# Float32r list matmuls, and the first two row gathers issued in the routing block

## The chip, the cores and the metric

One NeuronCore of a Trainium2 chip runs the whole program. The metric is the device time of one execution in microseconds (us); lower is better. The kernel before takes 1667.98 us, the median of 3 runs (1664.65 to 1668.8).

## The reference, cut to what matters

A two-layer decoder trunk for 512 tokens of width 1024. Each layer has a mixer (layer 0: retention and pooling; layer 1: sparse attention over selected keys), a layer norm, a mixture of 32 experts with exact top-2 dispatch, a layer norm, and a gated injection. The change lies in the dispatch of the mixture of experts, which each layer does once:

```python
g_logits = (xt @ w_group) + b_group            # 4 groups, top 1
e_logits = (xt @ w_expert) + b_expert          # 8 experts in the group, top 2
gate     = g_w[:, None] * softmax(top_v)
expert   = grp[:, None] * EXPERTS_PER_GROUP + top_i
order    = argsort(flat_e)                     # (token, expert) pairs by expert
...
h = xt[tok] @ w_gu[e];  a, b = split(h, 2)     # per block of rows of one expert
ys = (silu(a) * b) @ w_down[e]
y  = zeros.at[row_tok].add(ys * row_gate)      # back to the tokens
```

All of it is float32. The lists (which token rows an expert reads, and where its results go) are whole numbers.

## The kernel before, in words

The program is a row of blocks. In a block each engine has its own stream of instructions, and semaphores order them. A block closes with a barrier of all engines: GpSimd (POOL) collects the arrivals of the other four engines and then releases them; after it, POOL alone clears the semaphores of earlier blocks (L79, `Stages.end`), and the next block starts. So an engine that arrives late, POOL too, holds all others.

For each layer `layer_end` calls two blocks, `route(l)` and `experts(l, ...)`:

- **`route`** makes the lists. VectorE (DVE) picks group and experts from the router's logits, and forms a membership matrix; TensorE (PE) turns it into ranks with bf16 matmuls (L737 to L741). DVE then writes, for 8 columns `u` of pairs, a one-hot matrix RS of the rank (L829, 128x1024) and the table VALUES of token numbers (L818). Eight matmuls (L746) of 128x128 stationary RS and 128x64 moving VALUES, both float32, add up in the PSUM bank MP the rows that each slot of each expert takes (32 columns) and puts (32 columns). DVE copies them as integers to `rows` (L844), whose halves are the views `taken` and `put`. POOL has only two memsets in this block (L761, L762), ready long before. SyncE (SP) issues the load of the third expert's down weights (L442).
- **`experts`** goes through the 32 experts in 16 pairs, q = 0 and 1. For each expert POOL copies its column of `taken` to a small tile (L1337) and issues an indirect DMA that gathers its rows of x from the HBM tensor `x_rows` (L871): 128 half rows of 2 KB, 64 slots, where empty slots read nothing. PE transposes them (L883), ScalarE (ACT) copies the result (L917), PE multiplies with gate and up weights (L898, 32 records per expert), ACT and DVE form the gated product (L921, L924), PE transposes and multiplies with the down weights (L905, L912), ACT scales (L1477), and POOL scatters the result (L877).

At the start of `experts`, POOL issues the gathers of experts 0 and 1, then an indirect DMA that blanks a part (L1352), waits for DVE's list of further rows, and enters its loop. PE starts with eight float32 matmuls (L1409, RS by GATES) that give each slot's gate, and only then does it wait for the first gather and transpose it. DVE waits for these gates before `list_further` (L935 to L953) and further list work (L1055, L1058).

The weights come over SP's one DMA queue: 4 MB of gate and up weights (two halves) and 2 MB of down weights for each expert. There are three areas for them. The first three experts' weights are issued ahead, in the blocks before; the load for expert 3 waits until PE has read the first half of expert 0's weights (`gu_after(0, 3, 0, 1)`), and from there on each load waits for PE to be through with the weights that it replaces.

Of the kernel before, what the change touches and what calls it, by code (L numbers as in the profile page):

```python
# [13 lines left out]
F32 = mybir.dt.float32  # L14
F32R = mybir.dt.float32r
# [3 lines left out]
ALU = mybir.AluOpType  # L19
# [3 lines left out]
P = 128  # L23
SEQ = 512
D = 1024
T = SEQ // P
# [11 lines left out]
NE = NG * EPG  # L38
# [12 lines left out]
def build(nc, A, out):  # L51
    ctx = ExitStack()
    ctx.enter_context(nc.allow_non_contiguous_dma(reason="small vectors to one feature per partition"))
    with ctx:
        def sb(name, shape, dt=F32):
            return ctx.enter_context(nc.sbuf_tensor(name, shape, dt))

        def lasting(name):

            return ctx.enter_context(nc.semaphore(name))  # L60
# [21 lines left out]
        sem = Stages.new  # L82
# [4 lines left out]
        def three(ap, b):  # L87
            return ap.rearrange("p (a b) -> p a b", b=b)
# [3 lines left out]
        w2 = sb("w2", [P, 4096])  # L92
# [9 lines left out]
        half_col = sb("half_col", [P, 2])  # L102
# [510 lines left out]
        R = route_views()  # L613
# [91 lines left out]
        CP = PS[0:1, 3, 0:NE]  # L705
        MP = PS[:, 5, 0:2 * NE]
        GP = PS[:, 7, 0:NE]
        RS = three(w2[:, 3072:3072 + 2 * T * P], P)
        VALUES = three(w2[:, 1024:1024 + 2 * T * 2 * NE], 2 * NE)
        GATES = three(w2[:, 2048:2048 + 2 * T * NE], NE)  # L710

        def over_tiles(ap, n):

            return ap.rearrange("p (o e) -> p o e", o=1).broadcast_to([P, n, ap.shape[1]])

        def over_columns(ap, n):

            return ap.rearrange("p (t o) -> p t o", o=1).broadcast_to([P, ap.shape[1], n])

        def route(l):  # L720
            n = f"route{l}"
            s_gmax, s_gexp, s_diff, s_ex = sem(f"{n}_gmax"), sem(f"{n}_gexp"), sem(f"{n}_diff"), sem(f"{n}_ex")
            s_member, s_rank = sem(f"{n}_member"), sem(f"{n}_rank")
            s_values, s_slots = sem(f"{n}_values"), sem(f"{n}_slots")
            s_zero = sem(f"{n}_zero")
            with nc.Block() as block:
                @block.sync
                def _(sp):
                    load_third_dn(sp, l)

                @block.tensor
                def _(pe):

                    pe.wait_ge(s_member, 1)
                    for t in range(T):
                        for u in range(t):
                            pe.matmul(RK[:, t, :], ones[:, :], R["M"][:, u, :], start=(u == 0), stop=False)  # L737
                        m = pe.matmul(RK[:, t, :], tri[:, :], R["M"][:, t, :], start=(t == 0), stop=True)
                    m.then_inc(s_rank, 1)
                    for t in range(T):  # L740
                        m = pe.matmul(CP, ones[:, 0:1], R["M"][:, t, :], start=(t == 0), stop=(t == T - 1))  # L741
                    m.then_inc(s_rank, 1)

                    pe.wait_ge(s_values, 1)
                    for u in range(2 * T):
                        m = pe.matmul(MP, RS[:, u, :], VALUES[:, u, :], start=(u == 0), stop=(u == 2 * T - 1))  # L746
                    m.then_inc(s_slots, 1)

                @block.scalar
# [9 lines left out]
                @block.gpsimd  # L759
                def _(pool):  # L760
                    pool.memset(w2[:, 0:1024], 0.0).then_inc(s_zero, 1)  # L761
                    pool.memset(R["zeros"], 0.0).then_inc(s_zero, 1)  # L762
                    pool.wait_ge(s_zero, 2)

                @block.vector
                def _(dve):
                    own = Own(dve, f"{n}_own")
# [55 lines left out]
                    for j in range(2):  # L823
# [2 lines left out]
                    own.wait()  # L826
                    pos = R["pos"].rearrange("p j t -> p (j t)")
                    own.done(dve.tensor_reduce(pos, R["rank"], AX.X, ALU.add))
                    dve.tensor_tensor(RS, over_tiles(R["slot"], 2 * T), over_columns(pos, P), ALU.is_equal)\  # L829
                       .then_inc(s_values, 1)  # L830

                    dve.wait_ge(s_gexp, T)
# [8 lines left out]
                    own.mark(dve.tensor_copy(entry[:, :, 2], gates))  # L841

                    dve.wait_ge(s_slots, 1)
                    own.mark(dve.scalar_tensor_tensor(R["rows"], MP, 2.0,  # L844
                                                      half_col[:, 1:2].broadcast_to([P, 2 * NE]), ALU.mult, ALU.add))
                    own.wait()
            Stages.end()


# [13 lines left out]
        def wait_alone(eng, semaphore, value, tick):  # L863


            eng.wait_ge(semaphore, value)
            eng.sem_inc(tick, 1)

        def gather(pool, q, index, s):

            pool.indirect_dma_start(out=xg[q], out_offset=None, in_=x_half,  # L871
                                    in_offset=bass.IndirectOffsetOnAxis(ap=index, axis=0),
                                    bounds_check=2 * SEQ - 1, oob_is_err=False).then_inc(s, 16)
# [177 lines left out]
        def place_last(dve, own, e, placed):  # L1051

            OH, W = R["OH"], R["last"]
            for t in range(T):
                own.mark(dve.tensor_scalar(W[:, t, :], RS[:, t, :], OH[:, t, e:e + 1], None, ALU.mult))  # L1055
            own.wait()
            for t in range(T):
                own.mark(dve.scalar_tensor_tensor(W[:, t, :], RS[:, T + t, :], OH[:, T + t, e:e + 1], W[:, t, :],  # L1058
                                                  ALU.mult, ALU.add))
# [189 lines left out]
                            xs = X[:, t - 2, c * NB:(c + 1) * NB]  # L1249
                            dve.tensor_tensor(xs, xs, sig[u % 4], ALU.add).then_inc(self.s_done, 1)  # L1250

        def experts(l, inj):

            n = f"moe{l}"
# [13 lines left out]
            def both(name, new=sem):  # L1270
                return [new(f"{n}_{name}{q}") for q in range(2)]

            s_take, s_gath, s_turn, s_xe = both("take"), both("gath", lasting), both("turn"), both("xe")
            s_gu_half = both("gu_half")
            s_gu, s_silu, s_gated, s_gturn = both("gu"), both("silu"), both("gated"), both("gturn")
            sp_tick, pool_tick = sem(f"{n}_sp_tick"), sem(f"{n}_pool_tick")
# [6 lines left out]
            with nc.Block() as block:  # L1283
# [47 lines left out]

                @block.gpsimd
                def _(pool):
                    def take_rows(q, i, first=False):
                        if not first:
                            wait_alone(pool, s_turn[q], i, pool_tick)
                        pool.tensor_copy(take1[q], R["taken"][:, bass.ds(expert(q, i), 1)])\  # L1337
                            .then_inc(s_take[q], 1)
                        wait_alone(pool, s_take[q], i + 1, pool_tick)
                        gather(pool, q, take1[q], s_gath[q])  # L1340

                    def put_rows(q, i):
                        wait_alone(pool, s_y[q], i + 1, pool_tick)
                        pool.tensor_copy(put1[q], R["put"][:, bass.ds(expert(q, i), 1)]).then_inc(s_put[q], 1)  # L1344
                        wait_alone(pool, s_put[q], i + 1, pool_tick)
                        scatter(pool, q, put1[q], s_scat[q])

                    take_rows(0, 0, first=True)
                    take_rows(1, 0, first=True)
                    pool.tensor_copy(put_none, R["put"][:, LAST:LAST + 1]).then_inc(s_none, 1)  # L1350
                    pool.wait_ge(s_none, 1)
                    pool.indirect_dma_start(out=y_rows, out_offset=bass.IndirectOffsetOnAxis(ap=put_none, axis=0),  # L1352
                                            in_=R["zeros"], in_offset=None, bounds_check=4 * SEQ - 1,
                                            oob_is_err=False).then_inc(s_blank, 16)
                    more = further.count(pool)
                    with pool.Fori(0, PAIRS - 1) as i:
                        for q in range(2):
                            take_rows(q, i + 1)
                            put_rows(q, i)
                    put_rows(0, PAIRS - 1)  # L1360
                    pool.wait_ge(s_scat[0], 16 * PAIRS)
                    pool.wait_ge(s_scat[1], 16 * (PAIRS - 1))
                    pool.wait_ge(s_blank, 16)

                    def fill_table():
                        pool.wait_ge(s_place, 1)
                        for c in range(2 * T):
                            pool.indirect_dma_start(
                                out=table, out_offset=bass.IndirectOffsetOnAxis(ap=R["place"][:, c:c + 1], axis=0),
                                in_=R["entry"][:, c, :], in_offset=None).then_inc(s_tab, 16)  # L1370
                        pool.wait_ge(s_tab, 16 * 2 * T)
                    further.pool(pool, more, fill_table)
# [566 lines left out]
        s_wg = [[lasting(f"s_wg{l}{c}") for c in range(2)] for l in range(2)]  # L1939
# [15 lines left out]
            return then_load  # L1955

        def layer_end(l, loads, after_tile, turn_after):
            route(l)
            experts(l, Injection(l, s_wg[l], loads, after_tile, turn_after))

        def next_layer_loads(sp, norm):
            load_latent_weights(sp)
# [63 lines left out]
```

## Time and profile before

| | |
|---|---|
| median of 3 runs | 1667.98 us (1664.65 to 1668.8) |
| profiled execution | 1662.05 us, of which the span of instructions is 1660.2 us |
| PE busy | 86% of the span |
| DVE, ACT, POOL busy | 25%, 18%, 11% |
| HBM traffic | 300 GB/s over the span; 425 to 431 GB/s in most of both experts blocks |
| chain that ended last | PE 19%, DMA 12%, issue 1%, ACT 1% |

Shares are of the span. The chain starts in the second layer, since it can be followed back only to about 1099 us. A "record" is one hardware pass that the profile shows; one matmul of the source may give one or two. PEclk 0.50 is TensorE's lower clock level, 1.2 GHz, and 1.00 the upper one, 2.4 GHz. L12 is line 12 of the kernel before; the same code lies 8 to 11 lines further down in the changed kernel.

### The profile page before, as it was taken

What the parts mean: (1) busy time and instruction counts of PE and PEld (TensorE: products, weight loads), DVE (VectorE), ACT (ScalarE), POOL (GpSimd) and SP (SyncE); (2) the same over time, 40 slices, a digit from 0 to 9 for tenths busy, and PEclk for the clock granted to TensorE, in tenths of its full rate; (3) what the DMA queues carried; (4) which work ended last, traced back from release to release, by engine and by line L of the source; (5) the groups of instructions that cost most, each with busy time, mean ns of one, the idle gap of its engine ahead of it and who ended that gap; (6) DMA issues with size and microseconds to landing.
All of it is one profiled execution on the core that took longest, in us unless ns stands there. A gap on an engine that the chain in (4) does not pass through costs nothing. (4 is left out here: it accounts for less than half of the span.)

```text
span 1660.2 us, 16843 instructions
## 1 busy us (share of the span) xinstructions
PE 1435.3 (86%) x6032; PEld 656.7 (40%) x6032; DVE 406.8 (25%) x1016; ACT 305.6 (18%) x622; POOL 188.8 (11%) x317
## 2 busy tenths in 40 slices
PE   6998978998888789879999989959988788889887
PEld 5885443332223233224444454533322223333333
DVE  3424341000000011044068353340000000011072
ACT  3212011111011011012234563011111011101121
POOL 0000001221111111100000221011111111111100
PEclk9999978999999999999999999969999999999999
DMA  7106357999999999994200004279999999999840
GB/s 283 51 26 266 139 201 314 396 427 430 429 428 429 428 429 428 425 376 165 108 1 1 1 2 187 122 304 385 429 429 428 431 429 428 429 428 426 362 189 38
DMA packets 78305, 482.55 MB, mean 291 GB/s; under 512 B 18400, under 2 KB 20452, under 8 KB 45480
## 3 DMA queue, kind: packets, MB, share of 16 engines
q1 hardware_dynamic: 65800, 463.76, 67.2%
q0 software_dynamic: 10240, 16.82, 2.7%
q10 hardware_dynamic: 2208, 1.20, 0.2%
q8 instruction: 37, 0.61, 0.1%
q14 instruction: 20, 0.16, 0.0%
HBM read 474.91 MB, written 23.59 MB: 300 GB/s over the span
## 5 line engine op out<-in xcount | busy, mean ns | idle before, releaser
L898 PE MATMUL PS<-wide,w 128*64 128x512 f32 x1984 | 447.3, 600 | 47.6 <-ACT w L917 29.0
L912 PE MATMUL PS<-slim,w 128*64 128x512 f32 x992 | 256.2, 663 | 77.4 <-issue 76.1
L898 PEld LDWEIGHTS PS<-wide,w 128*64 128x64 f32 x1984 | 136.6, 137 | 326.5 <-issue 259.5
L912 PEld LDWEIGHTS PS<-slim,w 128*64 128x64 f32 x992 | 85.0, 150 | 242.8 <-issue 240.6
L924 DVE TENSOR_TENSOR w<-w,PS 128x256 f32<-128x256 f32 x64 | 26.9, 421 | 530.9 <-ACT w L921 530.9
L1164 PE MATMUL PS<-wide,XT 128*128 128x512 f32 x256 | 116.5, 612 | 2.3 <-ACT XT L169 2.3
L921 ACT ACTIVATE w<-PS 128x256 f32<-128x256 f32 x64 | 24.6, 384 | 498.9 <-PE PS L898 498.9
L927 DVE COPY w<-PS 128x256 f32<-128x256 f32 x64 | 27.2, 425 | 300.0 <-PE PS L905 300.0
L1477 ACT ACTIVATE w<-PS,w 128x512 f32<-128x512 f32 x62 | 42.6, 688 | 315.2 <-PE PS L912 315.2
L1344 POOL COPY w<-w 128x1 uint32 (+1 forms) x62 | 11.3, 182 | 656.7 <-ACT w L1477 656.7
L1164 PEld LDWEIGHTS PS<-wide,XT 128*128 128x128 f32 x256 | 49.3, 196 | 62.8 <-issue 59.6
L871 POOL DMA_INDIRECT w<-x_rows,w x64 | 67.2, 1050 | 55.0 <-POOL w L1337 53.7
L877 POOL DMA_INDIRECT y_rows<-w x62 | 63.6, 1027 | 54.8 <-POOL w L1344 54.8
L639 PE MATMUL PS<-wide,slim 128*128 128x512 f32 x128 | 56.0, 594 | 1.1 <-PEq L1840 1.1
L883 PE MATMUL PS<-ident,w 128*128 128x128 f32 x256 | 42.8, 291 | 8.3 <-DMA w<-x_rows,w 8.2
L169 ACT ACTIVATE XT<-PS 128x512 f32<-128x512 f32 x40 | 21.7, 594 | 149.6 <-PE PS L162 149.6
L917 ACT ACTIVATE w<-PS 128x512 f32<-128x512 f32 x64 | 38.2, 597 | 44.5 <-PE PS L883 42.8
L405 PE MATMUL PS<-x_high,w_high 128*128 128x512 f32 x96 | 38.2, 398 | 8.1 <-DVE w_low L343 8.1
L905 PEld LDWEIGHTS PS<-ident,w 128*128 128x128 f32 x128 | 20.1, 206 | 56.7 <-issue 53.0
L1935 POOL TENSOR_SCALAR w<-w 128x512 f32<-128x512 f32 (+3 forms) x48 | 26.6, 555 | 128.2 <-DVE w L1899 127.7
L883 PEld LDWEIGHTS PS<-ident,w 128*128 128x128 f32 x256 | 36.8, 211 | 9.4 <-DMA w<-x_rows,w 9.4
L1919 ACT ACTIVATE w<-w 128x512 f32<-128x512 f32 (+3 forms) x64 | 35.6, 556 | 23.9 <-DVE w L1893 23.7
(225 smaller groups left out, 1494.5 us busy)
## 6 DMA issues: line engine op xcount, KB each, us to landing
wide<-in_moe_w_gu SPq DMA_DIRECT2D x124, 2048.0 KB, 25.4
slim<-in_moe_w_down SPq DMA_DIRECT2D x62, 2048.0 KB, 25.4
w<-in_moe_w_gu SPq DMA_DIRECT2D x4, 2048.0 KB, 18.7
wide<-in_ple_w_gate SPq DMA_DIRECT2D x4, 2048.0 KB, 13.8
w<-in_ab_w_in SPq DMA_DIRECT2D x2, 2048.0 KB, 14.0
w_in<-in_ab_w_in SPq DMA_DIRECT2D x2, 2048.0 KB, 7.5
x_rows<-X SPq DMA_DIRECT2D x8, 512.0 KB, 2.8
XT<-in_moe_w_down SPq DMA_DIRECT2D x2, 2048.0 KB, 20.8
```

Source lines behind the costliest of these rows:

```text
L405: m = pe.matmul(PS[:, j % 8, :], lhsT, rhs, start=(k == 0 and r == 0), stop=(k == KD - 1 and r == 2))
L639: m = pe.matmul(PS[:, 2 * t + c, :], mixed[:, k, t * P:(t + 1) * P], w_halves[c][:, k, :], start=(k == 0), stop=(k == KD - 1))
L871: pool.indirect_dma_start(out=xg[q], out_offset=None, in_=x_half, in_offset=bass.IndirectOffsetOnAxis(ap=index, axis=0), bounds_check=2 * ...
L877: pool.indirect_dma_start(out=y_rows, out_offset=bass.IndirectOffsetOnAxis(ap=index, axis=0), in_=ys[q], in_offset=None, bounds_check=4 * ...
L883: m = pe.transpose(PS[:, q, c * P:(c + 1) * P], xg[q].rearrange("p (f c) -> p c f", c=4)[:, c, :], ident[:, :])
L898: m = pe.matmul(PS[u * SLOTS:(u + 1) * SLOTS, 2 + q, :], xeT[q][:, k, :], gu[k].rearrange("p (a u c) -> p a u c", a=2, u=2)[:, :, u, :], s ...
L912: m = pe.matmul(PS[u * SLOTS:(u + 1) * SLOTS, 6 + q, :], gT[:, k, :], dn[k][:, u * NB:(u + 1) * NB], start=(k == 0), stop=(k == FF // P - 1))
L917: return act.activation(xeT[q].rearrange("p (u c) s -> p c u s", u=2), PS[:, q, :].rearrange("p (c u s) -> p c u s", c=4, u=2), ACT.Copy)
L927: return dve.tensor_copy(gT.rearrange("p (u c) s -> p c u s", u=2), PS[:, 4 + q, 0:2 * P].rearrange("p (c u s) -> p c u s", c=2, u=2))
L1164: m = pe.matmul(PS[:, self.gate_bank(u), :], XT[:, k, t * P:(t + 1) * P], WG[:, k, c * NB:(c + 1) * NB], start=(k == 0), stop=(k == KD - 1))
L1477: act.activation(ys[q], PS[:, 6 + q, :], ACT.Copy, scale=R["gate_of"][:, bass.ds(expert(q, i), 1)]).then_inc(s_y[q], 1)
L1919: act.activation(g, g, ACT.Exp, bias=nmax[:, i:i + 1], scale=-1.0, accum_out=rsum[:, i:i + 1]).then_inc(s_p, 1)
```

## The change

It has three parts, in both layers.

1. RS and VALUES get float32r views of the same memory (tiles `ranks` and `values`). The DVE instructions that write them write float32r, and the eight list matmuls read float32r. The gate matmuls and the further list work go on reading the same bytes of RS as float32.
2. L844 signals a semaphore of its own, `s_listed`. POOL waits for it in the routing block and issues both first gathers there, with the two columns of `taken` themselves as index, without the copies to the small tile.
3. The experts block on POOL thus starts with the blanking DMA. The gathers' semaphores are made before `route`. The copy counter of `take_rows` now starts one lower.

```diff
-        RS = three(w2[:, 3072:3072 + 2 * T * P], P)
-        VALUES = three(w2[:, 1024:1024 + 2 * T * 2 * NE], 2 * NE)
+        ranks = again("ranks", "w2", 3072, 2 * T * P)[:, :]
+        RANKS, RS = three(ranks, P), three(ranks.bitcast(F32), P)
+        VALUES = three(again("values", "w2", 1024, 2 * T * 2 * NE)[:, :], 2 * NE)
...
-                        m = pe.matmul(MP, RS[:, u, :], VALUES[:, u, :], start=(u == 0), stop=(u == 2 * T - 1))
+                        m = pe.matmul(MP, RANKS[:, u, :], VALUES[:, u, :], start=(u == 0), stop=(u == 2 * T - 1))
...
                     pool.wait_ge(s_zero, 2)
+                    pool.wait_ge(s_listed, 1)
+                    for q in range(2):
+                        gather(pool, q, R["taken"][:, q:q + 1], s_gath[q])
...
-                    dve.tensor_tensor(RS, over_tiles(R["slot"], 2 * T), over_columns(pos, P), ALU.is_equal)\
+                    dve.tensor_tensor(RANKS, over_tiles(R["slot"], 2 * T), over_columns(pos, P), ALU.is_equal)\
                        .then_inc(s_values, 1)
...
-                    own.mark(dve.scalar_tensor_tensor(R["rows"], MP, 2.0,
-                                                      half_col[:, 1:2].broadcast_to([P, 2 * NE]), ALU.mult, ALU.add))
-                    own.wait()
+                    dve.scalar_tensor_tensor(R["rows"], MP, 2.0, half_col[:, 1:2].broadcast_to([P, 2 * NE]),
+                                             ALU.mult, ALU.add).then_inc(s_listed, 1)
+                    dve.wait_ge(s_listed, 1)
...
-                    def take_rows(q, i, first=False):
-                        if not first:
-                            wait_alone(pool, s_turn[q], i, pool_tick)
+                    def take_rows(q, i):
+                        wait_alone(pool, s_turn[q], i, pool_tick)
                         pool.tensor_copy(take1[q], R["taken"][:, bass.ds(expert(q, i), 1)])\
                             .then_inc(s_take[q], 1)
-                        wait_alone(pool, s_take[q], i + 1, pool_tick)
+                        wait_alone(pool, s_take[q], i, pool_tick)
                         gather(pool, q, take1[q], s_gath[q])
...
-                    take_rows(0, 0, first=True)
-                    take_rows(1, 0, first=True)
```

POOL's stream around the end of layer 0's routing block, before. L726 is the jump out of the routing block, the rows of L79 clear semaphores, and the first of them carries the barrier's wait for the other engines; `w` stands for the working areas w1 to w4.

```order
L762 MEMSET w 128x512
L726 UNCONDITIONAL_BRANCH [waits route0_zero]
L79 ISA [waits barrier_Pool_Activation_PE_DVE_SP_gather]
L79 ISA x9
L1332 UNCONDITIONAL_BRANCH
L1337 COPY w<-w 128x1
L871 DMA w<-x_rows,w 128x512 [waits moe0_take0]
L1337 COPY w<-w 128x1
L871 DMA w<-x_rows,w 128x512 [waits moe0_take1]
```

The same place in the changed kernel, with its own line numbers (L882 is the gather, L734 the jump out of the block, L86 the clearing).

```order
L770 MEMSET w 128x512
L882 DMA w<-x_rows,w 128x512 [waits route0_listed,route0_zero]
L882 DMA w<-x_rows,w 128x512
L734 UNCONDITIONAL_BRANCH
L86 ISA [waits barrier_Pool_Activation_PE_DVE_SP_gather]
L86 ISA x10
L1343 UNCONDITIONAL_BRANCH
L1358 COPY w<-w 128x1
```

Both gathers have moved from behind the barrier to ahead of it, and the two copies are gone.

PE's stream at the same border in the changed kernel; only the tiles' names differ from before (`w` for `values` and `ranks`).

```order
L754 MATMUL PS<-values,ranks 128x64 [waits route0_values]
L754 MATMUL PS<-values,ranks 128x64 x7
L734 UNCONDITIONAL_BRANCH
L1382 UNCONDITIONAL_BRANCH [waits barrier_Pool_Activation_PE_DVE_SP_release]
L1417 MATMUL PS<-w,ranks 128x32 x8
L894 MATMUL PS<-ident,w 128x128 [waits gath00]
```

Nothing moved on PE: the gate matmuls (L1417, before L1409) still stand behind the barrier's release, and ahead of the first transpose (L894, before L883).

## Rows read from the trace of the kernel before

**Rows 1.** The page: busy shares by engine; the chain that ended last, by line
```profile
PE 1435.3 (86%) x6032; PEld 656.7 (40%) x6032; DVE 406.8 (25%) x1016; ACT 305.6 (18%) x622; POOL 188.8 (11%) x317
...
DMA wide<-in_moe_w_gu 11%; PE PS L898 9%; PE PS L912 4%; PE PS L1164 3%; DMA w<-x_rows,w 1%; PE PS L1089 1%; PE PS L883 1%; PE PS L905 0%; ACT w L917 0%; PE PS L162 0%; PE PS L1153 0%; DVE X L202 0%; DVE stats L190 0%; DVE X L198 0%; DVE X L1237 0%
```

**Rows 2.** The chain in order of time: start, us, what
```profile
1100.30 0.78 issue
1101.08 6.07 DMA w<-x_rows,w
...
1213.62 24.86 DMA wide<-in_moe_w_gu
```

**Rows 3.** Timeline, layer 0: start, us, engine, line, operation, [idle before <-releaser]
```profile
244.27 3.67 PE L746 MATMUL PS<-w 128*128 128x64 f32 x16 [2.55 <-DVE w L829]
...
247.97 0.22 DVE L844 SCALAR_TENSOR_TENSOR w<-PS,half_col 128x64 uint32<-128x64 f32 x1 [2.47 <-PE PS L746]
...
248.74 3.59 PE L1409 MATMUL PS<-w 128*128 128x32 f32 x16 [0.80 <-PEq L726]
...
250.92 1.20 POOL L871 DMA_INDIRECT w<-x_rows,w  x1 [1.36 <-issue]
...
253.23 1.03 POOL L871 DMA_INDIRECT w<-x_rows,w  x1 [0.90 <-POOL w L1337]
...
255.70 1.13 PE L883 MATMUL PS<-ident,w 128*128 128x128 f32 x4 [3.37 <-DMA w<-x_rows,w]
...
257.52 9.19 PE L898 MATMUL PS<-wide,w 128*64 128x512 f32 x32 [0.69 <-ACT w L917]
```

**Rows 4.** Timeline, the same place in layer 1
```profile
1098.57 0.23 DVE L844 SCALAR_TENSOR_TENSOR w<-PS,half_col 128x64 uint32<-128x64 f32 x1 [2.47 <-PE PS L746]
...
1099.34 3.59 PE L1409 MATMUL PS<-w 128*128 128x32 f32 x16 [0.81 <-PEq L726]
...
1101.08 1.13 POOL L871 DMA_INDIRECT w<-x_rows,w  x1 [0.93 <-POOL w L1337]
...
1107.19 1.12 PE L883 MATMUL PS<-ident,w 128*128 128x128 f32 x4 [4.26 <-DMA w<-x_rows,w]
...
1109.01 8.41 PE L898 MATMUL PS<-wide,w 128*64 128x512 f32 x32 [0.69 <-ACT w L917]
```

**Rows 5.** Single lines: duration ns min/median/max, first and last start, form
```profile
L405 PE MATMUL PS<-x_high,w_high x96: 387/389/764, 19.1 to 85.6; 128*128 128x512 f32 x96
...
L343 DVE TENSOR_TENSOR w_low<-w_in,w_high x8: 1218/1756/2293, 17.8 to 93.5; 128x1024 fp32r<-128x1024 f32 x4, 128x2048 fp32r<-128x2048 f32 x4
...
L829 DVE TENSOR_TENSOR w<-w x2: 1224/1225/1226, 243.0 to 1093.6; 128x1024 f32<-128x1024 f32 x2
```

**Rows 6.** The gathers (L871) issued from 225 to 300 us: issue to landing
```profile
DMA to landing us min/median/max: 2.7/4.7/7.4
```

**Rows 7.** The three gathers (L871) issued from 1085 to 1120 us
```profile
DMA to landing us min/median/max: 3.4/4.0/6.1
```

**Rows 8.** The 21 gathers (L871) issued from 379 to 800 us
```profile
DMA to landing us min/median/max: 7.9/8.5/9.8
```

**Rows 9.** Stretches: length, busy us (instructions) by engine, PEclk, DMA share, GB/s
```profile
252.00:254.00 2.00, 0.33 (x2) 0.20 (x1) 1.49 (x8) 0.00 (x0) 1.09 (x3) 0.50 1.00 418
254.00:255.00 1.00, 0.00 (x0) 0.00 (x0) 0.93 (x4) 0.00 (x0) 0.45 (x2) 0.50 0.56 205
...
257.50:261.70 4.20, 4.18 (x10) 1.24 (x12) 0.87 (x4) 1.27 (x1) 1.06 (x2) 0.50 0.00 0
...
1105.00:1106.00 1.00, 0.00 (x0) 0.00 (x0) 0.93 (x4) 0.00 (x0) 0.66 (x1) 0.50 0.88 357
```

**Rows 10.** Timeline, layer 0: the first users of what the change delays
```profile
267.18 0.42 DVE L924 TENSOR_TENSOR w<-w,PS 128x256 f32<-128x256 f32 x1 [8.80 <-ACT w L921]
...
269.32 7.09 PE L898 MATMUL PS<-wide,w 128*64 128x512 f32 x32 [0.69 <-ACT w L917]
...
280.12 0.65 PE L883 MATMUL PS<-ident,w 128*128 128x128 f32 x4
```

More of the change, by code:

```diff
@@ L54, in build, with again @@
     with ctx:
+        home = {}
         def sb(name, shape, dt=F32):
+            home[name] = -(-nc.sbuf_base // 32) * 32
             return ctx.enter_context(nc.sbuf_tensor(name, shape, dt))
+        def again(name, of, first, n):
+            return nc.alloc_sbuf_tensor_at(name, [P, n], F32R, offset=home[of] + 4 * first)
         def lasting(name):
@@ L718, in over_columns, with route @@
             return ap.rearrange("p (t o) -> p t o", o=1).broadcast_to([P, ap.shape[1], n])
-        def route(l):
+        def route(l, s_gath):
             n = f"route{l}"
@@ L724, in route @@
             s_values, s_slots = sem(f"{n}_values"), sem(f"{n}_slots")
-            s_zero = sem(f"{n}_zero")
+            s_zero, s_listed = sem(f"{n}_zero"), sem(f"{n}_listed")
             with nc.Block() as block:
@@ L1250, in dve, with experts @@
                             dve.tensor_tensor(xs, xs, sig[u % 4], ALU.add).then_inc(self.s_done, 1)
-        def experts(l, inj):
+        def experts(l, s_gath, inj):
             n = f"moe{l}"
@@ L1271, in both @@
                 return [new(f"{n}_{name}{q}") for q in range(2)]
-            s_take, s_gath, s_turn, s_xe = both("take"), both("gath", lasting), both("turn"), both("xe")
+            s_take, s_turn, s_xe = both("take"), both("turn"), both("xe")
             s_gu_half = both("gu_half")
@@ L1957, in layer_end @@
         def layer_end(l, loads, after_tile, turn_after):
-            route(l)
-            experts(l, Injection(l, s_wg[l], loads, after_tile, turn_after))
+            s_gath = [lasting(f"gath{l}{q}") for q in range(2)]
+            route(l, s_gath)
+            experts(l, s_gath, Injection(l, s_wg[l], loads, after_tile, turn_after))
         def next_layer_loads(sp, norm):
```

## The prediction

> **What bounds the kernel now.** I read the page first. PE is busy for 86% of the span, and the chain that ended last is made of weight loads and PE's expert matmuls [rows 1]. This asks for the place where such a chain takes its start. The chain in order of time begins, in layer 1, with a gather: 0.78 us of issue, then 6.07 us from the gather's issue to its landing, then the first transpose, and PE from there on; weight loads decide only from 1213.62 us on [rows 2]. Before that PE runs without a longer wait, and SP's loads wait for PE, since an area is loaded anew when PE has read it. In layer 0 DMA is idle from 257.5 to 261.7 us, a stretch in which PE alone works [rows 9]. So the whole experts block, its load-bound middle included, hangs on the start of the first transpose. Each us by which it moves, in either layer, is a us of the total.
>
> Next I read the timeline just ahead of it. In layer 0 the list matmuls take 3.67 us for 16 records and L844 ends at 247.97 + 0.22 = 248.19. PE starts the gate matmuls at 248.74 and ends them at 252.33. The first gather starts only at 250.92, and PE waits 3.37 us for its landing, until 255.70 [rows 3]. In layer 1 L844 ends at 1098.80, the gather starts at 1101.08, and the transpose at 1107.19 after 4.26 us of idling [rows 4]. So what ends last there is the gather, and behind it, with 3.4 to 4.3 us of slack, the gate matmuls.
>
> **The change part by part.**
>
> *The list matmuls.* 16 records in 3.67 us, of which the last lasts 0.42 us, are (3.67 - 0.42) / 15 = 0.217 us each. That float32 makes two records per matmul is seen from 16 records for 8 matmuls. The float32r matmuls of L405 are 96 records in one group for 96 matmuls, one each [rows 5]. So 8 records go, 1.7 us per layer, all on the path (DVE waits for them before L844). The bounds are 0 (the record of float32r takes twice as long at only 64 moving columns, which no row here shows) and 1.7. I take 1.7: a 128x128 weight load stands ahead of each record in both types, and 0.217 us per record is what it sets. L844 would then end at 246.5 and 1097.1. The Trainium skill (FP8 and Floating Point Precision, section TensorE Precision Notes) says that true float32 takes four passes through the array, where reduced precision reads once. By it the estimate would be three quarters of 3.67, or 2.75 us, saved, and the sum 2 us larger; the trace has two records per matmul, not four, so the sum stands on the records.
>
> *DVE's writes as float32r.* Zero: L829 takes 1.22 us for 128x1024 in float32, and L343 1.22 us at its shortest, for 128x1024 in float32r [rows 5].
>
> *The first gather.* Removed ahead of it: the barrier, the clearing of semaphores, the copy and its wait. It started 2.73 us behind L844's end in layer 0 and 2.28 in layer 1 [rows 3, 4]. What stays is the 0.78 us of issue that stands ahead of an indirect DMA even where nothing is waited for [rows 2], and a semaphore's way from DVE to POOL, some 0.1 us. I take 0.9 us (from 0.1, no issue time, to 1.4, the longest idle in front of one [rows 3]). It starts at 247.4 and 1098.0, 3.5 and 3.1 us earlier.
>
> *Its landing* doesn't move by as much. In both layers SP's queue is still moving weights at full rate: the DMA share is 1.00 until 254 us and 0.56 in the microsecond after; in layer 1 it is still 0.88 from 1105 to 1106 [rows 9]. The first gathers landed 4.7 us (layer 0, the middle one of the row's three figures [rows 6]) and 6.1 us (layer 1, the last one [rows 7]) after their issue, each about a us behind the end of these loads. One into idle queues takes 2.7 us [rows 6], one into a queue that stays full 8.5 us in the middle of 21 [rows 8]. The earlier gathers meet 7 us of full queue. I take the middle of 6.1 and 8.5, 7.3 us, nearest to layer 1's; the ends are 2.7 and 8.5. They land at 254.7 and 1105.3.
>
> *The barrier.* The two gathers now stand ahead of it, so POOL holds all engines. First gather 0.9 + 1.2 us, second 0.8 of issue and 1.05: POOL arrives 3.95 us behind L844's end; without a second issue time 3.15. From L844's end to the gate matmuls' start it took 248.74 - 248.19 = 0.55 us before, which I add. They start at 4.5 us and end 3.6 us later, 8.1 us behind L844's end: 254.6 and 1105.2 (253.8 and 1104.4 by the shorter hold). Before they ended at 252.33: this is the new wait, nearly as late as the landing, and its cost lies in slack that was there.
>
> *What waits behind it.* DVE's further lists start with the gates, 2.3 us later; they ended 258.4 and end 260.6, and the first user of DVE is L924, at 267.18 before and 1 us earlier now [rows 10]. POOL's third gather, released by these lists, goes from 260.8 to 263.1; even at 8.5 us it lands at 271.6, and its transpose stands at 280.12 [rows 10], so 7 us of cover stay. The second gather is needed only with the second expert. The clear of one more semaphore runs beside PE. The weights on SP's queue that the gathers now overtake (0.25 MB each) are used over 10 us later. All zero.
>
> *Sum.* The first transpose starts at 254.7 instead of 255.70, and at 1105.3 instead of 1107.19: 1.0 + 1.9 = **2.9 us**. The profiled execution would go from 1662.05 to 1659.2 us. The median lies 5.9 us above that execution; I take the same difference from it: 1667.98 - 2.9 = **1665.1 us**, 0.17% less. A measurement of this kernel can tell about 0.3%, or 5 us, from no change.
>
> **The rivals.**
>
> *The gather isn't held up by the loads.* Then only the gate matmuls count, and if the second gather also goes out right behind the first, they end at 253.8 and 1104.4: 1.9 + 2.8 = 4.7 us, 1663.3. For it: the gathers of 8.5 us had a scatter ahead of them on POOL's queue, and these have nothing. Against: 6.1 us in layer 1 with only 5 us of full queue. The Trainium skill (DMA: Bandwidth & Descriptors, section Queues, rings and completion order) says that each DMA engine takes turns between queue rows, packet by packet, so a gather would not wait for the loads' end; by that rule this rival holds. The trace has landings of 8.5 us in a full queue that never empties, which agrees with turns, but slow ones.
>
> *It lands with the loads' end in any case.* At 8.5 us: 255.9, held to the old 255.7 by the empty queue, and 1106.5. 0 + 0.7 us, 1667.3.
>
> *The float32r matmuls save nothing.* Then L844 ends at 248.2 and 1098.8, the gates at 256.3 and 1106.9: +0.6 and -0.3, in sum 0.3 us slower, 1668.3. Against it: L405's single records.
>
> *Slower: the barrier.* If POOL can't issue the second gather before the first has landed, the gates end at 254.7 + 0.8 + 1.05 + 0.55 + 3.6 = 260.7 and 1111.3, which is 5.0 + 4.1 = 9.1 us later than before: 1677.1. It costs from the point where the gates start more than 5.6 us (layer 0) or 6.4 us (layer 1) behind L844's end, instead of 4.5. Against it: the second gather was issued at 253.23, before the first had landed [rows 3].
>
> *Slower: the clock.* PE's pause ahead of the gate matmuls grows from 0.80 us [rows 3] to some 4.6 us. The clock is at 1.2 GHz there anyway, and stays so for 4.2 us into L898 [rows 9], which takes 9.19 and 8.41 us instead of 7.09 [rows 3, 4, 10]. If the clock rose only after the whole first expert, L898 would take 14.2 us in each layer, 10.8 us more in sum, less 2.9: 1675.9. Each us by which the rise comes later costs 0.5 us, so 5.8 us in sum would undo the gain. If it came sooner than now, up to 2.1 + 1.3 us more would be won. Nothing here lengthens the pause directly ahead of L898, so I give neither much.
>
> **How the numbers follow.** Forecast 0.42, gather not held up 0.27, landing with the loads 0.13, float32r without gain 0.06, clock 0.05, barrier 0.04, anything else 0.03. Faster by over 0.3% needs 5 us: some of the second case, where the clock rises sooner too, and the spread of the runs (1664.65 to 1668.8) on top: 0.21. Slower by over 0.3% are the barrier and the clock: 0.08. The rest, 0.71, is within 0.3%. The range for 8 in 10 leaves out the two slow rivals. It reaches from the 4.7 us of the second case and 1.6 us for clock and spread, 1661.7, to the float32r rival and 0.5 us of spread, 1668.8.
>
> **What would show it.** L746's place: 8 records in about 1.95 us. DVE's L844 to the first indirect DMA: 0.9 us, with a start of the gate matmuls 4.5 us behind. The gather: 7.3 us to landing. PE's idle time before the first transpose: under 0.5 us in place of 3.4 and 4.3. From L844's end to the transpose 8.2 us in both layers, where it was 7.5 and 8.4. It would be wrong if landings come at 5 us or less (more gain), if the wait for the gates is longer than 5.6 us, or if L898's first group changes from 9.2 and 8.4 us by over a us.

## The result, and the profile after

The changed kernel takes 1672.2 us (median of 20 runs, 1667.58 to 1676.5) where the kernel before takes 1665.69 us (20 runs beside them, 1661.73 to 1672.85). The ratio is 1.0038, 95% interval 1.0028 to 1.0048: 6.3 us slower by the ratio (the interval is 4.7 to 8.0 us). Forecast were 2.9 us faster. The profiled execution took 1671.51 us, span 1669.6. The ratios here and below leave out two executions that were far slower than the others of their kernel, 1896.47 us (experiment 2, without the drain) and 2473.7 us (experiment 3).

The page of the changed kernel, its parts 1 and 4:

```profile
PE 1431.9 (86%) x6016; PEld 657.6 (39%) x6016; DVE 406.6 (24%) x1016; ACT 305.3 (18%) x622; POOL 187.7 (11%) x313
...
DMA wide<-in_moe_w_gu 11%; PE PS L909 9%; PE PS L923 4%; PE PS L1175 3%; PE PS L1100 1%; PE PS L894 1%; DMA w<-x_rows,w 1%; PE PS L916 0%; ACT w L928 0%; PE PS L169 0%; PE PS L1417 0%; PE PS L1164 0%; DVE X L209 0%; DVE stats L197 0%; DVE X L205 0%
```

Beside [rows 1] there are 16 PE records fewer, as meant, and one new entry: the gate matmuls (L1417, L1409 before) are now on the chain. The timeline shows why, in layer 0 (start, us, engine, line, operation, idle before and its releaser):

```profile
244.34 1.92 PE L754 MATMUL PS<-values,ranks 128*128 128x64 f32 x8 [2.55 <-DVE ranks L840]
...
246.30 0.23 DVE L855 SCALAR_TENSOR_TENSOR w<-PS,half_col 128x64 uint32<-128x64 f32 x1 [0.71 <-PE PS L754]
247.50 1.20 POOL L882 DMA_INDIRECT w<-x_rows,w  x1 [10.50 <-DVE w L855]
249.01 1.01 POOL L882 DMA_INDIRECT w<-x_rows,w  x1 [0.31 <-issue]
256.19 3.60 PE L1417 MATMUL PS<-w,ranks 128*128 128x32 f32 x16 [9.93 <-PEq L734]
...
259.60 1.09 PE L894 MATMUL PS<-ident,w 128*128 128x128 f32 x4
...
261.38 8.69 PE L909 MATMUL PS<-wide,w 128*64 128x512 f32 x32 [0.69 <-ACT w L928]
```

and in layer 1:

```profile
1102.80 0.22 DVE L855 SCALAR_TENSOR_TENSOR w<-PS,half_col 128x64 uint32<-128x64 f32 x1 [0.71 <-PE PS L754]
1103.92 1.13 POOL L882 DMA_INDIRECT w<-x_rows,w  x1 [9.94 <-DVE w L855]
1105.35 1.00 POOL L882 DMA_INDIRECT w<-x_rows,w  x1 [0.31 <-issue]
1112.83 3.59 PE L1417 MATMUL PS<-w,ranks 128*128 128x32 f32 x16 [10.07 <-PEq L734]
...
1116.23 1.09 PE L894 MATMUL PS<-ident,w 128*128 128x128 f32 x4
```

The lists come 1.75 us sooner (8 records in 1.92 us against 16 in 3.67 [rows 3]), and the first gather starts 0.97 us behind the end of the lists' copy, as predicted. But PE then stands still for 10 us. The second indirect DMA is over at 250.02, the gate matmuls start only at 256.19, and their releaser is the closing of the routing block (PEq L734). The transpose no longer waits for the gather: it follows the gate matmuls at once.

What POOL does meanwhile is not counted as busy. It stands in the records of its sequencer. First the line that closes the routing block in the kernel before, then the same line in the changed kernel (ns min/median/max, first and last start):

```profile
L726 POOLq DRAIN  x2: 34/34/34, 237.6 to 1088.2; - x2
```

```profile
L734 POOLq DRAIN  x2: 8112/8206/8300, 247.8 to 1104.2; - x2
```

A block is closed on each engine by a DRAIN ahead of the barrier. On POOL it took 0.03 us, and now it takes 8.1 and 8.3 us. In layer 0 it goes from 247.8 to 255.9, in layer 1 from 1104.2 to 1112.5. The gathers landed as follows (both of layer 0, then both of layer 1, us from issue):

```profile
DMA to landing us min/median/max: 6.8/6.9/7.1
```

```profile
DMA to landing us min/median/max: 6.7/6.9/7.1
```

The second gather of layer 0 landed at 249.0 + 6.8 = 255.8, and the drain ended 0.1 us later. In layer 1 the drain ended at 1104.2 + 8.3 = 1112.5, within 0.1 us of the second landing (1105.35 + 7.1). In both layers the gate matmuls start 0.4 us behind that landing. That the drain waits for the landings of DMAs that POOL has issued is the theory (A) that the experiments had to test.

For all kernels below I give the **approach**: the time from the routing block's first DVE instruction (L770, now L781: 234.9 and 1091.8 in the changed kernel) to the start of the first expert matmul (L898, now L909), read from each run's timeline. The experts block hangs on its end.

| kernel | approach, layer 0 | layer 1 | sum against before |
|---|---|---|---|
| before | 22.25 us | 23.44 us | |
| changed | 26.48 us | 26.17 us | +7.0 us |

That fits the measured 6.3 us, within its interval. The profiled executions differ by 9.5 us. The rest lies outside the change: from the first expert matmul of layer 0 to the routing block of layer 1 it is 828.0 us before and 830.5 after. In the runs of experiment 1 and in the first two of experiment 2, which alter nothing in that stretch, it is 827.6 to 835.8. So one profiled execution can differ from another by some us there, whatever the approach is.

### The profile page after: what moved, and what is told of

It reads as the page before. It is cut to its first block and busy times, and to the rows that moved or that the text cites. A ratio compares the mean times of both kernels' runs of the same rounds, so it can differ in the third digit from the quotient of the medians.

```text
span 1669.6 us, 16775 instructions
## 1 busy us (share of the span) xinstructions
PE 1431.9 (86%) x6016; PEld 657.6 (39%) x6016; DVE 406.6 (24%) x1016; ACT 305.3 (18%) x622; POOL 187.7 (11%) x313
## 5 line engine op out<-in xcount | busy, mean ns | idle before, releaser
L909 PE MATMUL PS<-wide,w 128*64 128x512 f32 x1984 | 446.9, 600 | 48.5 <-ACT w L928 29.7
L909 PEld LDWEIGHTS PS<-wide,w 128*64 128x64 f32 x1984 | 139.4, 137 | 324.3 <-issue 257.8
L938 DVE COPY w<-PS 128x256 f32<-128x256 f32 x64 | 27.2, 424 | 298.8 <-PE PS L916 298.8
L882 POOL DMA_INDIRECT w<-x_rows,w x64 | 67.2, 1049 | 72.0 <-POOL w L1347 51.0
L894 PE MATMUL PS<-ident,w 128*128 128x128 f32 x256 | 42.6, 290 | 0.7 <-DMA w<-x_rows,w 0.6
L916 PEld LDWEIGHTS PS<-ident,w 128*128 128x128 f32 x128 | 20.1, 206 | 56.4 <-issue 52.8
L1943 POOL TENSOR_SCALAR w<-w 128x512 f32<-128x512 f32 (+3 forms) x48 | 26.5, 553 | 129.9 <-DVE w L1907 129.5
L1901 DVE CUSTOM_DVE_ANT_0 w<-PS,w 128x512 f32<-128x512 f32 (+2 forms) x48 | 26.3, 552 | 53.3 <-PE PS L1858 53.2
```

What stands on the lines that cost most here:

```text
L894: m = pe.transpose(PS[:, q, c * P:(c + 1) * P], xg[q].rearrange("p (f c) -> p c f", c=4)[:, c, :], ident[:, :])
L909: m = pe.matmul(PS[u * SLOTS:(u + 1) * SLOTS, 2 + q, :], xeT[q][:, k, :], gu[k].rearrange("p (a u c) -> p a u c", a=2, u=2)[:, :, u, :], s ...
L938: return dve.tensor_copy(gT.rearrange("p (u c) s -> p c u s", u=2), PS[:, 4 + q, 0:2 * P].rearrange("p (c u s) -> p c u s", c=2, u=2))
```

## Experiments

**1. One part of the change at a time.** The float32r lists alone: the kernel before with `RANKS`, `VALUES` and L746 as in the change, the gathers where they were.

> Float32r list matmuls alone; both first gathers stay in the experts block as before. Theory A (the loss is the closing drain of the routing block on POOL, which waits for the gathers in flight): nothing is in flight here, so the drain is short, L844's end and all behind it come 1.7 us earlier per layer, and the first expert matmul 1 to 1.7 us earlier, since the landing is partly held by the weight loads. Sum 2 to 3.5 us faster than before. Theory B (float32r at 64 columns or the clock is at fault): no gain or slower than before.

Ratio 0.9993 (0.998 to 1.0006), approach 22.48 and 22.37 us, 0.8 us less in sum. The 2 to 3.5 us that theory A expected were missed: less than half is there by the approaches, and the time can't tell it from no gain. Its timeline in layer 0:

```profile
246.00 0.22 DVE L852 SCALAR_TENSOR_TENSOR w<-PS,half_col 128x64 uint32<-128x64 f32 x1 [0.71 <-PE PS L754]
246.77 3.59 PE L1417 MATMUL PS<-w,ranks 128*128 128x32 f32 x16 [0.80 <-PEq L734]
248.96 1.20 POOL L879 DMA_INDIRECT w<-x_rows,w  x1 [1.37 <-issue]
...
255.72 1.13 PE L891 MATMUL PS<-ident,w 128*128 128x128 f32 x4 [5.36 <-DMA w<-x_rows,w]
```

The gather goes out 2 us earlier than before and lands at the same time, 6.7 us behind its issue instead of 4.7. In this layer it is the forecast's rival "it lands with the loads' end in any case"; in layer 1 the approach is 1.1 us shorter. That float32r makes the kernel 6.3 us slower is refuted: the interval ends at 1.0006, 1 us.

The gathers alone: the change with the list matmuls left in float32.

> The gathers moved ahead of the barrier, but the list matmuls left in float32. Theory A (the hold lasts until the landings, and these are tied to the end of the weight loads): the lists are 1.7 us later than in the changed kernel, but the release of the barrier only 0 to 0.7 us, so the first expert matmul starts 26.5 to 27.2 us after the routing block's first DVE instruction; total 7 to 9 us slower than before. Theory B (the hold is a fixed time behind the lists' copy): 1.7 us later per layer than the changed kernel, 10 us slower than before.

Ratio 1.0041 (1.0026 to 1.0057), approach 28.00 and 26.78 us, +9.1 us in sum; 6.8 us slower in time. So the gathers' move is the whole loss. In layer 0 the approach is 1.5 us longer than in the changed kernel and in layer 1 0.6 us; expected were 26.5 to 27.2 us, which layer 0 misses. Layer 1 fits a hold up to a landing that the loads set, layer 0 fits a landing 7.0 us behind the issue. The intervals of the two kernels overlap, and this one rests on 4 runs.

**2. The drain.** The changed kernel, closed without POOL's drain. The barrier stays, and so do the drains of the other four engines, by the rows of its trace.

```diff
-            with nc.Block() as block:
+            with nc.Block(no_gpsimd_drain=True) as block:
```

> The changed kernel, with the routing block closed without POOL's drain (the barrier stays). Theory A: the gate matmuls start about 4 us behind the end of the lists' copy (9.7 us in the changed kernel), the first expert matmul 21.5 us (layer 0) and 20.7 us (layer 1) after the routing block's first DVE instruction, where before it was 22.3 and 23.5 and in the changed kernel 26.5 and 26.2. Total 3.5 us faster than before, 10 us faster than the changed kernel. Theory B (POOL is held by issuing the gathers, or the barrier itself is slow with them): the gate matmuls still start 9 to 10 us behind, time as in the changed kernel.

Ratio 0.9984 (0.9966 to 1.0002), approach 21.19 and 20.99 us against the expected 21.5 and 20.7; 10.5 us less than the changed kernel in sum, and 9 us less by the two ratios. Against the kernel before the approaches are 3.5 us shorter; the time says 2.7 us, with an interval that just includes no change. Layer 0:

```profile
246.09 0.22 DVE L855 SCALAR_TENSOR_TENSOR w<-PS,half_col 128x64 uint32<-128x64 f32 x1 [0.71 <-PE PS L754]
247.29 1.20 POOL L882 DMA_INDIRECT w<-x_rows,w  x1 [10.02 <-DVE w L855]
247.84 3.59 PE L1417 MATMUL PS<-w,ranks 128*128 128x32 f32 x16 [1.78 <-PEq L734]
248.80 1.01 POOL L882 DMA_INDIRECT w<-x_rows,w  x1 [0.31 <-issue]
...
254.52 1.13 PE L894 MATMUL PS<-ident,w 128*128 128x128 f32 x4 [3.09 <-DMA w<-x_rows,w]
```

The gate matmuls start 1.53 us behind the lists' copy (1.77 in layer 1), where theory A had expected about 4, even before the second gather runs on POOL. So POOL's sequencer passes the barrier ahead of the work that it has handed on, and the second gather's issue holds nobody; theory B falls. Before the change it was 0.55 us; where the added 1.0 and 1.2 us come from isn't shown. What is left is the wait for the gather, landed 7.2 us behind its issue.

Then two explicit waits in the drain's place:

```diff
+                    for q in range(2):
+                        pool.wait_ge(s_gath[q], 16)
```

> The changed kernel without POOL's drain, but with two explicit waits on the gathers' semaphores in its place, at the end of POOL's part of the routing block. Theory A (the drain lasts until both gathers have landed): the same time as the changed kernel within 1 us, gate matmuls 9.5 to 10 us behind the end of the lists' copy. Theory B (the drain waits for something shorter or longer than the landings): a difference of 2 us or more between this and the changed kernel.

```profile
243.54 0.23 DVE L857 SCALAR_TENSOR_TENSOR w<-PS,half_col 128x64 uint32<-128x64 f32 x1 [0.71 <-PE PS L754]
...
246.25 1.01 POOL L884 DMA_INDIRECT w<-x_rows,w  x1 [0.30 <-issue]
...
253.89 3.60 PE L1419 MATMUL PS<-w,ranks 128*128 128x32 f32 x16 [10.39 <-PEq L734]
```

The second gather lands 7.2 us behind its issue, at 253.45, and the gate matmuls start 0.4 us later, 10.1 us behind the copy. Approach 26.50 and 26.17 us, to 0.02 us that of the changed kernel. The ratio 1.0062 (1.004 to 1.0085) is 4 us above that of the changed kernel, where within 1 us was expected; the two intervals overlap narrowly, and these are only 6 runs. In the timeline a wait for both landings does what the drain does.

With only the first gather ahead of the barrier:

> The changed kernel with only the first gather ahead of the barrier, the second in the experts block. Theory A: POOL's drain ends with the landing of the one gather, 7.2 us behind its issue; gate matmuls start 19.4 us, first expert matmul 24.8 us after the routing block's first DVE instruction (26.5 and 26.2 in the changed kernel), total 3 to 5 us slower than before. Theory B (two gathers issued back to back are what POOL's drain can't get through): the drain is short, the first expert matmul starts at 21 us, 2 to 3 us faster than before.

```profile
L734 POOLq DRAIN  x2: 6814/7049/7284, 245.6 to 1105.7; - x2
```

The drain is 0.8 and 1.5 us shorter: it begins with one gather's issue and ends with one landing (7.0 us behind the issue in layer 0, 6.5 in layer 1). Gate matmuls 19.5 and 19.0 us in, approach 24.65 and 24.13 us, as theory A has it. The ratio is 1.001 (0.9999 to 1.0022), or 1.7 us slower, less than the 3.1 us of the approaches and under the expected 3 to 5. One gather in flight already brings the hold; that it takes two is refuted.

**3. Work under the hold.** The gate matmuls moved to the end of PE's part of the routing block, the drain left in:

```diff
                     m.then_inc(s_slots, 1)
+                    pe.wait_ge(s_gated_in, 1)
+                    for u in range(2 * T):
+                        m = pe.matmul(GP, RS[:, u, :], GATES[:, u, :], start=(u == 0), stop=(u == 2 * T - 1))
+                    m.then_inc(s_gates, 1)
```

> The changed kernel with the eight gate matmuls moved from the start of the experts block to the end of PE's part of the routing block; POOL's drain stays. Theory A: the gate matmuls run under the drain, and the first transpose starts right at the barrier's release, 21.3 and 21.0 us after the routing block's first DVE instruction; the first expert matmul 23.1 and 22.8 us after it. That is 3.6 us per layer less than in the changed kernel, and the same as before within 1 us. Theory B (the gather's landing is late, the barrier is not what counts): the gate matmuls were not on the path, time as in the changed kernel.

Ratio 0.9999 (0.9983 to 1.0015), approach 22.93 and 22.66 us (expected 23.1 and 22.8), which is 3.5 us per layer less than in the changed kernel.

```profile
255.73 1.10 PE L899 MATMUL PS<-ident,w 128*128 128x128 f32 x4 [6.78 <-PEq L735]
```

The transpose now waits for the barrier alone. The loss is thus two things in a row: the hold until the landing, and 3.6 us of gate matmuls, which before ran under the gather's flight and after the change behind it.

**4. What holds the landing.** Theory A2: the weight loads on SP's queue do. Its rival B2: the landing takes that long whatever else is under way. In the kernel before, the third expert's down weights (2 MB) are issued only behind both landings; nothing else changes:

```diff
-                    load_third_dn(sp, l)
+                    pass
...
+                    for q in range(2):
+                        sp.wait_ge(s_gath[q], 16)
+                    load_third_dn(sp, l)
                     more = further.count(sp)
```

> The kernel before, with the third expert's down weights issued only when both first gathers have landed, and nothing else. Theory A2: the gathers meet an empty queue and land 2.7 to 3.4 us behind their issue, in place of 4.7 and 6.1; first expert matmul 20.2 to 20.8 us after the routing block's first DVE instruction; total 4 to 5 us faster than before. Theory B2: no change.

Ratio 0.9965 (0.9952 to 0.9978), approach 20.72 and 20.37 us. The two first gathers of layer 0 and of layer 1:

```profile
DMA to landing us min/median/max: 2.8/3.0/3.2
```

```profile
DMA to landing us min/median/max: 2.8/2.9/3.0
```

The first landed 4.7 and 6.1 us behind its issue before, and 3.2 and 3.0 here. B2 falls. The ratio is 5.8 us faster, where 4 to 5 were expected. The Trainium skill (DMA: Bandwidth & Descriptors, section Anatomy of one DMA — SWDGE (gpsimd) path) gives such a DMA about 2.0 us plus its bytes at 436 GB/s, an estimate of 2.6 us for 0.25 MB. These rows agree within 0.6 us, while the gathers ahead of the barrier, beside the weight loads, took 5.9 to 7.2 us in the runs with this load in its old place, which that fit leaves out.

The changed kernel without the drain and with this load late:

> The changed kernel without POOL's drain at the end of the routing block, and with the third expert's down weights (2 MB, L442) issued by SyncE only when both first gathers have landed. Theory A2 (with the drain gone, the first transpose waits for a gather that the weight loads ahead of it hold up): the weight loads end 4.9 us earlier, the gather lands 3 to 4.5 us behind its issue in place of 7.2, the gate matmuls become the last wait, and the first expert matmul starts 18.2 us (layer 0) and 18.6 us (layer 1) after the routing block's first DVE instruction; 22.3 and 23.4 before. Total 8 to 9 us faster than before. Theory B2 (the landing takes 7 us whatever else is under way): 21.2 and 21.0 us as with the drain removed alone, 2 to 3.5 us faster than before.

Ratio 0.9933 (0.9919 to 0.9948): 11 us faster than before, where 8 to 9 were expected. Approach 18.44 and 19.43 us (expected 18.2 and 18.6). Layer 0:

```profile
245.63 1.20 POOL L882 DMA_INDIRECT w<-x_rows,w  x1 [10.01 <-DVE w L855]
246.19 3.59 PE L1420 MATMUL PS<-w,ranks 128*128 128x32 f32 x16 [1.78 <-PEq L734]
...
250.12 1.13 PE L894 MATMUL PS<-ident,w 128*128 128x128 f32 x4 [0.34 <-DMA w<-x_rows,w]
```

The transpose now waits only 0.34 us for the gather, 1.07 us in layer 1. The first gather lands 4.4 and 5.2 us behind its issue, not 3: it goes out earlier than in the run before, while the other weight loads are still under way. This version beats both kernels.

Last, the same load late, but with the drain left in:

> The changed kernel with POOL's drain in place, and the third expert's down weights issued only when both first gathers have landed. Theory A (the hold is the landing time and nothing else): with the second gather landing 3.8 us (layer 0) and 4.7 us (layer 1) behind its issue, as without the drain, the barrier's release moves to 17.6 and 18.6 us after the routing block's first DVE instruction (21.3 and 21.0 in the changed kernel), the first expert matmul to 23.0 and 24.0 us; total 1 to 2 us slower than before and 5 to 6 us faster than the changed kernel. Theory B (the drain has a price of its own, 8 us): release still at 21 us, time as in the changed kernel.

```profile
L734 POOLq DRAIN  x2: 4229/5230/6232, 246.5 to 1096.4; - x2
```

The drain shrinks with the landings (4.1 and 2.9 us for the two gathers of layer 0, 6.3 and 5.0 for those of layer 1): it has no price of its own. The gate matmuls start at 16.95 and 18.91 us, approach 22.14 and 24.09 us (expected 17.6 and 18.6, 23.0 and 24.0). The time does not fit as well: the ratio 0.9981 (0.9971 to 0.9991) is 3.2 us faster than before, where the approaches say 0.5 us slower and 1 to 2 us slower was expected. In the run before it (drain away, load late) it was 11 us against 7.8 by the approaches, and with the load late alone 5.8 against 4.6. So the late load may be worth 1 to 4 us more somewhere else, or the approaches of one execution don't stand for the runs: the profiled execution of the kernel before is 3.6 us below its median, that of the kernel with one gather ahead 6.3 us above. This stays open.

## Why the prediction was wrong

**What bounds the kernel** held. The approach to the first expert matmul carries over nearly one to one in the changed kernel, +7.0 us there and 6.3 us in the time; in the experiments the two differ by up to 4 us.

**The list matmuls, DVE's writes, the gather's start** held: 1.92 us for 8 records (1.95 forecast), L840 at 1.22 us in float32r, and 0.97 and 0.90 us from the lists' copy to the gather (0.9). The Trainium skill (FP8 and Floating Point Precision, section TensorE Precision Notes) gives true float32 four passes; against one for float32r, that would by an estimate have saved 2.75 us per layer. The trace has 1.75, one half and not three quarters.

**The landing** held: 7.1 us in layer 0 and 6.7 in layer 1, forecast 7.3. That it came so close is partly luck, since the forecast took the middle of 6.1 and 8.5 us, two rows of different load. Experiments 1 and 4 show the load as its cause.

**The step that failed is "The barrier".** It said: "POOL arrives 3.95 us behind L844's end", and the gate matmuls "start at 4.5 us". They started 9.7 us (256.19 - 246.53) and 9.8 us (1112.83 - 1103.02) behind it. The sum of issue times was the wrong quantity. With the drain, the hold ends 0.4 us behind the landing of the last gather; without it, it is 1.5 and 1.8 us, and the gate matmuls start before POOL's second indirect DMA has begun. The rest of the forecast's picture then comes out: in that run the approaches are 1.1 and 2.5 us shorter than before, where 1.0 and 1.9 us were forecast. The forecast described the barrier only as a meeting of engines. The kernel before has the drain in its sequencer rows at 0.03 us, with nothing in flight; no row priced it with a DMA in flight, and the forecast gave no bound for that.

The rival "Slower: the barrier" had the place and the turning point (5.6 and 6.4 us from the copy to the gate matmuls), but as mechanism a second gather that can't be issued before the first lands. The second was issued 1.5 us behind the first. It priced a hold of 10.6 us in both layers at 9.1 us. With the measured 9.7 and 9.8 us, its own turning points give 4.1 + 3.4 = 7.5 us, near the 7.0 of the approaches. With 0.04 it had too small a chance, and the range left it out.

**The cover for the gate matmuls** was seen as slack of 3.4 to 4.3 us. It went with the hold: 3.6 us per layer came onto the path, and experiment 3 gives 3.5 of it back.

**The clock** did not decide. L909 took 8.69 and 8.75 us for the first expert of the two layers, against 9.19 and 8.41 before: 0.2 us less in sum. The base did not decide either: the forecast's 1665.1 us stood on a median of 3 runs, 2.3 us above that of 20, and the change itself is missed by 9.2 us.

## What to carry to other kernels

Before a DMA is moved ahead of the end of a block, look at what closes the block on the engine that issues it: a drain there turns "issued early" into "everyone waits until it has landed". The row to read is the sequencer's DRAIN, and in this kernel its length is the landing time under the load of that moment, not the issue time. And an early request gains only what the queues beside it leave: here 2 MB of weights, which PE first reads at 300.50 us, 50 us behind the start of the first gather, cost the kernel before 1.5 and 3.1 us of landing.

## What the runs showed of the hardware

- POOL's DRAIN lasted 8.1 and 8.3 us with two gathers in flight in the changed kernel (7.1 to 8.4 us in the other runs with two in flight and the weight load in its old place), 6.8 and 7.3 us with one, 4.2 and 6.2 us with two and the late load, and 0.03 us with none. In every run with gathers in flight it ended within 0.2 us of the last landing.
- Without the drain, PE passed the barrier 1.5 and 1.8 us behind the lists' copy, while POOL's second indirect DMA had not begun: the barrier doesn't order behind the work that POOL's sequencer has handed on.
- Two indirect DMAs in a row have 0.30 to 0.31 us between them, where 0.80 to 0.93 us stood when a copy and its wait came between.
- A gather of 128 half rows (0.25 MB) takes 2.8 to 3.2 us from issue to landing with the third expert's load late and the gathers behind the barrier, 2.9 to 6.3 us with it late and the gathers ahead of it, and 5.9 to 7.2 us ahead of it beside that load.
